# A hybrid attention and expert layer: the latents' projection pieces in halves, two merge gates moved into the attention

## The reference, cut to what matters

```python
u = x * (1 + sc1) + sh1
xc, bg, cg, q, k, v, g_conv, g_na = jnp.split(u @ w_in, IN_SPLITS, axis=-1)
y_conv = short_conv(xc, bg, cg, conv_w)          # three taps along the tokens, then times bg
...                                              # q, k, v by heads; context: plain attention
y_na = neighbourhood_attention(q, k, v, k_ctx, v_ctx, rpb)   # latents: window + cached keys
merged = (jax.nn.sigmoid(g_conv) * (y_conv @ w_conv_out) +
          jax.nn.sigmoid(g_na) * (y_na @ w_na_out))
x = layer_norm(ALPHA * x + ga1 * (merged @ w_o), ln1_g, ln1_b)
u2 = x * (1 + sc2) + sh2
# peer: each token picks 128 of 16384 experts; a = gelu(<expert_u row, u2>) * gate; y = sum of a * expert_v row
x = layer_norm(ALPHA * x + ga2 * peer(u2, ...), ln2_g, ln2_b)
```

## Time and profile before

| what | us |
|---|---|
| median of three runs (lowest, highest) | 1871.84 (1871.19, 1873.35) |
| the profiled execution, its own time | 1869.3 |
| its span, first to last instruction | 1867.5 |
| PE busy (share of the span) | 1767.4 (95%) |
| DVE busy | 1268.5 (68%) |
| POOL busy | 899.0 (48%) |
| ACT busy | 296.7 (16%) |
| latents' attention, first scores to first gate | 307.06 to 458.25 |
| latents' merge, first gate to output projection | 458.25 to 626.15 |
| dense stages | from 811 on |

### The profile page before, as it was taken

One profiled execution on the slowest core, in us unless ns is written; L12 is line 12 of the kernel. 1 busy time (PEld: TensorE's weight loads), 2 busy tenths in 40 slices (PEclk: granted clock), 3 DMA queues, 4 the chain that ended last, 5 costly groups with the idle time before them and its releaser, 6 DMA issues.

```text
span 1867.5 us, 20547 instructions
## 1 busy us (share of the span) xinstructions
PE 1767.4 (95%) x7508; PEld 1103.2 (59%) x7508; DVE 1268.5 (68%) x2592; ACT 296.7 (16%) x669; POOL 899.0 (48%) x838
## 2 busy tenths in 40 slices
PE   5988999998999999999999999998889999999995
PEld 3674844454444467678888888886544434444442
DVE  1212569888579798989889888878855533236767
ACT  0120012554100011111100100117620000000000
POOL 1000337656456323254555756576855654435541
PEclk9999999999999999999999999999999999999998
DMA  9998679889999887789999999998989999999995
GB/s 394 412 348 330 244 234 393 301 322 322 362 358 409 352 298 284 252 331 353 371 387 389 409 400 406 402 407 294 354 326 409 409 409 409 409 409 409 409 410 224
DMA packets 171204, 670.15 MB, mean 359 GB/s; under 512 B 19770, under 2 KB 20922, under 8 KB 166364
## 3 DMA queue, kind: packets, MB, share of 16 engines
q0 software_dynamic: 112368, 409.74, 57.7%
q1 hardware_dynamic: 53984, 243.29, 33.3%
q10 hardware_dynamic: 4752, 15.81, 2.2%
HBM read 659.27 MB, written 7.39 MB: 357 GB/s over the span
## 4 chain that ended last, share of the span: by engine, by line
PE 74%; DVE 11%; DMA 6%; POOL 5%; issue 3%; ACT 1%; SPq 1%; DVEq 0%; ACTq 0%; POOLq 0%
PE psum L978 24%; PE psum L1052 21%; DVE psum L1968 5%; PE psum L1150 4%; POOL arena L639 4%; PE psum L835 4%; PE psum L824 3%; DMA arena<-in_expert_v_dram,arena 3%; PE psum L1173 3%; PE psum L1076 2%; PE psum L1079 2%; PE psum L1005 2%; PE psum L810 2%; PE psum L1113 1%; PE psum L821 1%
## 5 line engine op out<-in xcount | busy, mean ns | idle before, releaser
L639 POOL DMA_INDIRECT arena<-in_expert_u_dram,arena x384 | 473.9, 1234 | 339.0 <-DVE arena L1677 212.6
L1677 DVE CUSTOM_DVE_ANT_0 arena<-arena 128x1024 f32<-128x1024 f32 x384 | 459.5, 1221 | 150.9 <-DMA arena<-in_expert_u_dram,arena 149.3
L639 POOL DMA_INDIRECT arena<-in_expert_v_dram,arena x384 | 376.7, 981 | 359.8 <-DVE psum L1968 197.2
L1968 DVE SCALAR_TENSOR_TENSOR psum<-arena,psum 128x1024 f32<-128x1024 f32 x254 | 327.0, 1287 | 186.3 <-DMA arena<-in_expert_v_dram,arena 172.8
L1052 PE MATMUL psum<-arena 128*128 128x512 f32 x1024 | 444.1, 595 | 0.0
L978 PE MATMUL psum<-arena 128*128 128x256 f32 x2048 | 442.6, 379 | 0.0
L978 PEld LDWEIGHTS psum<-arena 128*128 128x128 f32 x2048 | 388.8, 190 | 52.8
L1052 PEld LDWEIGHTS psum<-arena 128*128 128x128 f32 x1024 | 194.0, 190 | 251.0 <-issue 251.0
L1471 ACT ACTIVATE arena<-psum 128x512 f32<-128x512 f32 x64 | 38.2, 597 | 383.5 <-PE psum L978 383.5
L835 PE MATMUL psum<-arena 128*128 128x512 f32 x192 | 87.7, 610 | 0.8 <-ACT arena L1258 0.8
L1150 PE MATMUL psum<-arena 128*128 128x384 f32 x256 | 85.2, 486 | 0.0
(11 more groups left out here) (200 smaller groups left out, 1476.0 us busy)
## 6 DMA issues: line engine op xcount, KB each, us to landing
arena<-in_expert_uT_dram SPq DMA_DIRECT2D x128, 512.0 KB, 6.9
arena<-in_expert_v_dram SPq DMA_DIRECT2D x128, 512.0 KB, 6.8
arena<-in_w_ada_dram SPq DMA_DIRECT2D x12, 2048.0 KB, 13.8
arena<-in_w_in_dram SPq DMA_DIRECT2D x11, 2048.0 KB, 11.3
arena<-in_w_query_dram SPq DMA_DIRECT2D x8, 2048.0 KB, 11.2
arena<-in_w_in_dram SPq DMA_DIRECT2D x30, 512.0 KB, 8.1
arena<-in_w_o_dram SPq DMA_DIRECT2D x16, 512.0 KB, 6.6
arena<-in_expert_u_dram,arena POOLq DMA_INDIRECT x384, 9.1
```

The source lines that it names most:

```text
L639: pool.indirect_dma_start(slot, None, table[0], bass.IndirectOffsetOnAxis(ap=number, axis=0)).then_inc(land, 16)
L1677: dve.tensor_tensor_reduce(UR[b], UR[b], U2B[e], 1.0, 0.0, ALU.mult, ALU.add, DOTS[e % 2][:, k:k + 1]).then_inc(u_free, 1)
L1968: dve.scalar_tensor_tensor(ys, row, weight, ys, ALU.mult, ALU.add).then_inc(v_free, 1)
```

## The change

`HALVES` gives each of the 14 first iterations one or two halves of a piece: 2, 2, 1, 1 and so on, so the same 22 halves are spread without an empty iteration. The first gate of step 8 is computed in halves into bank 5 after iterations 14 and 15, the first gate of step 9 whole into bank 0 after iteration 16. In the merge, step 8 then computes both attention gates (banks 1 and 4), step 9 none; ACT takes these four banks with two sigmoids a step. `PAIR_ROWS` falls by 8 in all, and in an iteration with a convolution the third row would come after it; `MERGE_ROWS` rises by 4 in steps 8 and 9. ACT's Gelu and the five parameter loads follow the sigmoid of step 10. The diff, with what is left out marked:

```diff
-PIECE_AFTER = {0: 1, 1: 2, 2: 3, 4: 4, 5: 5, 6: 6, 8: 7, 9: 8, 10: 9, 12: 10, 13: 11}
+HALVES = (2, 2, 1, 1, 2, 2, 1, 1, 2, 2, 1, 1, 2, 2)
+HALVES_TO = [2 + sum(HALVES[:i]) for i in range(len(HALVES) + 1)]
+PIECE_AFTER = {i: [m for m in range(1, 12) if HALVES_TO[i] <= 2 * m + 1 < HALVES_TO[i + 1]] for i in range(len(HALVES))}
+GATE_HALVES, GATE_NEXT = {14: 0, 15: 1}, 16
+GATE_BANKS = {8: (5, 1), 9: (0, 4)}
...
-            def project_piece(m):
+            def project_half(n):
+                m, half = divmod(n, 2)
...
+                if half == 0:
+                    weights(pe, ("conv", 1, c))
+                    pe.wait_ge(proj_out, PROJ_QKV + m)
+                for k in range(4 * half, 4 * half + 4):
+                    mm = pe.matmul(bank(5), own[:, k, :], UT[:, k, CTX:NT], start=k == 0, stop=k == KD - 1)
+                if half == 1:
+                    mm.then_inc(proj_done, 1)
+            def first_gate(half):
+                wc = merge_weights(pe, "gconv", 1, 0, 0)
+                if half == 0:
+                    pe.wait_ge(proj_out, PROJ_QKV + 12)
+                for k in range(4 * half, 4 * half + 4):
+                    pe.matmul(bank(5), wc[:, k, :], UT[:, k, CTX:NT], start=k == 0, stop=k == KD - 1)
+            def second_gate():
+                wc = merge_weights(pe, "gconv", 1, 0, 1)
+                pe.wait_ge(win_step, NU - 2)
                 for k in range(KD):
+                    pe.matmul(bank(0), wc[:, k, :], UT[:, k, CTX:NT], start=k == 0, stop=k == KD - 1)
...
-                    if i in PIECE_AFTER:
-                        project_piece(PIECE_AFTER[i])
+                    if i < len(HALVES):
+                        for half in range(HALVES_TO[i], HALVES_TO[i + 1]):
+                            project_half(half)
+                    if i in GATE_HALVES:
+                        first_gate(GATE_HALVES[i])
+                    if i == GATE_NEXT:
+                        second_gate()
...
+                        if d not in GATE_BANKS:
+                            wc = merge_weights(pe, "gconv", s, hf, c)
...
+                        for at_once in {8: (8, 9), 9: ()}.get(d, (d,)):
+                            wn = merge_weights(pe, "gna", s, hf, at_once % 4)
+                            own = bank(GATE_BANKS[at_once][1] if at_once in GATE_BANKS else 1)
...
+                            mm.then_inc(gates_done, 1)
...
-                else:
-                    act.wait_ge(win_step, NU - 2)
...
+                    if d in GATE_BANKS:
+                        act.activation(SG[s][:, 0, :], bank(GATE_BANKS[d][0]), ACT.Sigmoid)
+                        act.activation(SG[s][:, 1, :], bank(GATE_BANKS[d][1]), ACT.Sigmoid).then_inc(sig_out, 1)
...
-                    if s == 1 and i == WEIGH_STEP:
+                    if s == 1 and i == WEIGH_STEP + 1:
                         weigh(0)
+                    if s == 1 and i == ROWS_STEP:
+                        load_rows(s)
...
-                    context_rows(rows - 2)
                     if i in CONV_AFTER:
                         convolve_piece(CONV_AFTER[i])
+                    context_rows(max(rows - 2, 0))
...
-PAIR_ROWS = (6, 6, 4, 2, 6, 6, 4, 2, 6, 6, 4, 2, 6, 6, 2, 2)
+PAIR_ROWS = (6, 6, 1, 3, 6, 6, 1, 3, 6, 6, 1, 3, 6, 6, 1, 1)
-MERGE_ROWS, NORM_ROWS = (8, 8, 14, 14, 14, 14, 12, 3), 4
+MERGE_ROWS, NORM_ROWS = (12, 12, 14, 14, 14, 14, 12, 3), 4
+ROWS_STEP = 2
```

More of the change, by code:

```diff
@@ L951, in latent_attention @@
             def latent_attention():
-                project_piece(0)
+                project_half(0)
+                project_half(1)
                 for i, n in enumerate(range(2, NU + 4, 2)):
@@ L1073, in section @@
                             pe.wait_ge(sig_out, d)
[L1074 to L1081, removed]
+                        if d not in GATE_BANKS:
+                            wc = merge_weights(pe, "gconv", s, hf, c)
+                            for k in range(KD):
+                                pe.matmul(bank(0)[:, 0:n_tok], wc[:, k, :], UT[:, k, tok], start=k == 0, stop=k == KD - 1)
+                        for at_once in {8: (8, 9), 9: ()}.get(d, (d,)):
+                            wn = merge_weights(pe, "gna", s, hf, at_once % 4)
+                            own = bank(GATE_BANKS[at_once][1] if at_once in GATE_BANKS else 1)
+                            for k in range(KD):
+                                mm = pe.matmul(own[:, 0:n_tok], wn[:, k, :], UT[:, k, tok], start=k == 0,
+                                               stop=k == KD - 1)
+                            mm.then_inc(gates_done, 1)
                         if d >= 1:
@@ L1345, in latent_attention @@
                         take_out(n - 3)
-                    if i in PIECE_AFTER:
-                        take_piece(PIECE_AFTER[i])
+                    for m in PIECE_AFTER.get(i, ()):
+                        take_piece(m)
             def normalise(n):
@@ L1358, in load_x, with load_rows @@
                 act.dma_start(XB[min(e, 1)], rows(x_prompt, x_sample, e)).then_inc(xb_in, 16)
+            def load_rows(s):
+                own = mods_d[s:s + 1, :]
+                for n, row in ((0, own[:, 2 * D:3 * D]), (1, ln1_g[0:1, :]), (2, ln1_b[0:1, :]),
+                               (3, own[:, 4 * D:5 * D]), (4, own[:, 3 * D:4 * D])):
+                    act.dma_start(PRM[s][n], row.partition_broadcast(P)).then_inc(prm_in[s], 16)
             def section(s):
@@ L1374, in section @@
                         act.wait_ge(merge_step, 2 * d)
-                    src = bank(0, 2).rearrange("p (a b) -> p a b", a=2)[:, :, 0:n_tok]
-                    act.activation(SG[s], src, ACT.Sigmoid).then_inc(sig_out, 1)
-                    if s == 1 and i == WEIGH_STEP:
+                    if d in GATE_BANKS:
+                        act.activation(SG[s][:, 0, :], bank(GATE_BANKS[d][0]), ACT.Sigmoid)
+                        act.activation(SG[s][:, 1, :], bank(GATE_BANKS[d][1]), ACT.Sigmoid).then_inc(sig_out, 1)
+                    else:
+                        src = bank(0, 2).rearrange("p (a b) -> p a b", a=2)[:, :, 0:n_tok]
+                        act.activation(SG[s], src, ACT.Sigmoid).then_inc(sig_out, 1)
+                    if s == 1 and i == WEIGH_STEP + 1:
                         weigh(0)
+                    if s == 1 and i == ROWS_STEP:
+                        load_rows(s)
                 if s == 0:
```

4 lines of the change are left out of this document (removed).

## The result

| | before | after |
|---|---|---|
| median of 7 runs each, us | 1871.19 (1867.29 to 1873.35) | 1877.05 (1874.79 to 1883.37) |
| profiled execution; its span | 1869.3; 1867.5 | 1874.8; 1873.0 |
| ratio after to before | | 1.0042, interval 1.0026 to 1.0059 |

The kernel became slower, by 0.42% (7.9 us of 1871.19, 4.9 to 11 by the interval; the two medians lie 5.9 apart). The forecast was 1863.0 in 1855 to 1869, with 5% for slower. It was wrong.

The account below looks back on a forecast made before the run. PE was taken to bound the merge's first three steps, DVE the rest, with the DMA near its ceiling. Terms 8.4 + 9.9 - 4.0 - 5.5 = 8.8 took 1871.84 to 1863.0, range 1855 to 1869.

Parts of the forecast that it names:

- What bounds, and the attention: PE bounds the merge's first three steps, DVE the rest; halves and early gates start the merge 8.4 us earlier.
- Rival D: Attention: the halves leave the stall where it was, 5.9 of the gain lost, total gain 2.9, 1868.9; chance 6%.
- Steps 11 to 15: Later merge steps: as before, no term in the sum; the weights' order on SP only gets earlier.
- the eight rows' feed: Merge: score rows moved out of the attention must be fetched while DVE runs; cost 4.0, bounds 0 and 7.7.
- rival C: Merge score rows: POOL's fetch instructions, not the DMA, feed them, 18.2 late; slower, 1877.2; chance 5%.
- rival B: Merge: the feed eats the gain, rows 7.7 late and loads 10; gain 0.6, 1871.2, no change; chance 13%.
- The check by bytes: 72.4 MB to the last merge step: gain 21.6 at 410 GB/s, 3.6 at the old average; the forecast needs 382.
- the loads: Five parameter loads moved to step 10, 2.62 MB, delay value rows there; cost 5.5, bounds 0 and 10.
- the 0.46 at 569.53: A DVE wait in the merge's value rows before the change, read as a sign of no DMA slack.
- 9.9: Merge steps 8 to 10: gain with two gates less on PE, if the rows are there; 52.3 instead of 62.2.
- step 10 later than S + 60: Sign of a wrong forecast: this product over 60 us after the merge's start S would blame the scores' feed.
- Waits over 10 in the value rows: Sign of a wrong forecast: DVE waits of this size in the merge would blame the five moved loads.

Follow-up runs that it names:

- e6: The halves alone, with gates, parameter loads and Gelu as in the kernel before and the eight rows in the attention: 1861.74, ratio 0.9935 to the kernel before.
- e1: The changed kernel with the query weight loads held back on SP until the merge's last product: 1871.99, ratio 1.0004 to the kernel before.
- e8: The kernel before with the query weight loads held back until the merge's last product: 1871.16, ratio 0.9990.
- e10: The changed kernel with 24 score rows of steps 8 and 9 as products with PSUM, their sums left out: 1876.56, ratio 1.0036 to the kernel before.
- e3: The changed kernel with query weights held back and the five parameter loads ahead of step 8: 1864.08, ratio 0.9958 to the kernel before.
- e2: The changed kernel with the five parameter loads issued ahead of step 8 again: 1871.22, ratio 1.0001 to the kernel before.
- e5: e3 with the eight rows back in the attention: 1852.01, ratio 0.9892 to the kernel before.
- e9: e5 without the hold on the query weight loads: 1856.78, ratio 0.9932 to the kernel before.
- e4: e3 with eight score rows of steps 8 and 9 done ahead of step 8: 1867.54, ratio 0.9988 to the kernel before.

## Why the prediction was wrong

*What bounds, and the attention: right.* 7.7 of 8.4 earlier, with one wait of 0.42 left. Rival D (halves don't fill the holes) is out, by e6 as well.

*The first failure, the largest in the forecast: "Steps 11 to 15. As before (520.42 to 624.16), no term. The weights' order on SP only gets earlier."* The second sentence was the cost, not a comfort. PE has two gates (13.7) less to do in the merge, while DVE is held up by rows. PE's rest ahead of the output projection was 2.83 and is 11.41 when the weights are held back (e1); its slots come free 10.7 earlier on the clock (612.67 for 623.35), and SP fills them with 4 MB under the last rows. That costs 8.6, shown by e1, and brings the rest to 20.55; it was not there before, by e8. What releases SP's next issue, and what it would then meet, was not asked.

*The second, a term mis-sized: the eight rows' feed, taken at 4.0 with bounds 0 to 7.7, measured 8.1.* The price per row came from fetches at 1.28 and 1.56 apart; they were 1.75 apart. That is rival C's mechanism (2.29 a row, and 1.95 to decide), and e10 shows that it is worth 2. The other 6 are rival B's, a late feed, of which no run shows how much is bytes: in 471 to 485 the DMA stood at 270 GB/s, since the first fetch comes only when DVE frees a buffer at 475.29, and in e10, with POOL fast, it is full from 485 on. The check by bytes asked whether 382 GB/s on average can be had. It can (403 in e3), but an average doesn't tell when in the stretch the bytes are wanted. The 387 that S to step 15 reached in the changed kernel hold the query weights besides.

*The third term, the loads, was right in kind:* 7.8 for 5.5, in its bounds, all between the products of steps 10 and 12. e2 shows it. One sign for it was misread: the 0.46 at 569.53 is no wait for a row.

*Sum by measured terms:* 7.7 + 9.9 - 8.1 - 7.8 - 8.6 = -6.9. Two things come beside it. In PE's 20.55 of rest the granted clock falls, and it is still low when the output projection starts at 633.19:

```profile
625.00:649.00 24.00, 15.81 (x31) 6.99 (x32) 8.17 (x7) 0.00 (x0) 4.70 (x5) 0.72 0.74 298
```

The granted clock is 0.50, the 1.2 GHz level, in 633 to 637 and full from 639 on (0.72 on average over 625 to 649), and the first 64 matmuls take 30.41 where they took 27.73 before. A shorter rest need not give that back: after 3.79 in e5 they take 30.42, after 2.83 in e6 27.73. This 2.7 is still there at the start of the dense stage (189.4 behind the output projection's start, 186.7 before). Behind that the changed kernel is 4.2 shorter, 3.3 of it in the dense stage and its gathering (564.4 for 567.7), which differs as much between e5 and e9 (563.3 and 567.7), whose code is the same there. No cause was shown for that.

*The range was too narrow at the top* since each term had its bounds but the term left out had none, and the rows' feed came out above its bound (8.1 for 7.7). That freed slots draw transfers forward was in no rival. Rival C's time, 1877.2, is the measured one by luck: its mechanism was to cost 18.2 and cost 2, and the loads and the query weights made up the rest. Of the signs that the prediction named, step 10 later than S + 60 was right to point at the scores' feed. Waits over 10 in the value rows would have blamed the loads alone, though 8.9 of them are the query weights'.

## What to carry to other kernels

Taking work from an engine that leads makes it lead by more, and a transfer that waits for its buffers can move forward with it: look up what that transfer will stand beside, and hold it, so that it doesn't meet the feed of the engine that bounds (e1), or leave the other engine less to lead by (e9). A free stretch of an engine that eats rows is room for more rows only if the DMA has room there too (e4). Undo a change part by part: here the halves alone were good for 0.65% (e6), the halves and the gates for 1.1% (e5), and what came with them (eight rows, five loads, query weights set free) cost 1.5%.

## What the runs showed of the hardware

One core's DMA moved 403 to 413 GB/s when several queues were full, and 422 over 612 to 633. A 512 KB row landed 8.1 after its issue (median) with q0 at 80.8% of the engines' time and 17.7 beside SP's weights. A fetch instruction on POOL takes 0.94 alone or beside one-input work, up to 1.99 beside two-input score rows. And single executions differ by up to 5.4 in the time of the first scores (307.1 to 312.5) among kernels whose code does the same until there, so the spans of two profiles can't be compared to better than that. The stretch from the first scores to the output projection can: it is 319.1 before and 319.2 in e8, whose merge is the same.
